# Second attention: 64-row scores of an even and an odd head issued in pairs, without zeroed queries

## The chip, the cores and the metric

One core of one Trainium2 chip. The metric is the time of the program on the device in microseconds. The kernel before ran three times: median 1390.95 us, from 1390.49 to 1391.43.

## The reference, cut to what matters

Three layers run over one sequence of 256 tokens of width 1024: an attention layer with latent projections (MLA), a MoBA attention layer, and a third layer of gated linear attention beside grouped-query attention, followed by a mixture of 64 experts. The change touches the attention of the second layer. With 256 tokens there is one key block, so that what counts of it is plain causal attention of 16 heads of 64 values:

```python
s_own = jnp.einsum('bhcd,bhkd->bhck', qq, k_own).astype(jnp.float32) * scale
s_own = jnp.where(k_pos[None, :] <= q_pos[:, None], s_own, -jnp.inf)
p = jax.nn.softmax(jnp.concatenate([s_sel, s_own], axis=-1), axis=-1).astype(qq.dtype)
...
return (o * jax.nn.silu(gate)) @ w_o
```

Each score is a sum over 64 values, half of the 128 rows of the TensorE array.

## The kernel before, in words

The program is written as one instruction stream for each engine, with semaphores between them; nothing is reordered by a planner. The order on every engine is the order of the lines that it runs.

**Work of an attention.** `attention(kind, ...)` (L1831 for TensorE, L1246 for VectorE, `softmax_units`, L841, for ScalarE) runs over units; a unit is one head and one tile of 128 queries. Kind "a" is the first attention, "b" the second (32 units: 0 to 15 are the 16 heads of tile 0 with 128 keys, 16 to 31 those of tile 1 with 256 keys), "g" the third (16 units, all with 256 keys). In loop step u TensorE issues
- the scores of unit u (L1840, one fp32 product, which the trace shows as two matmuls), and for "a" and "b" a bf16 matmul of the identity with the causal mask onto the last 128 keys (L1842, all 128 rows),
- the transposes of the probabilities of unit u-3 (L1768, after the exponentials of that unit),
- what is written beside this step: transposes of mixed outputs and pieces of the output projection (`project_piece`, L1813), in 15 steps from 18 to 35,
- the product of probabilities and values of unit u-4 (L1867, after VectorE has copied the transposed probabilities).

VectorE in step u takes the row maximum of the scores of unit u (L1252), then copies the transposed probabilities of unit u-3 to SBUF (L1076), then what is written beside (splits of weights, L1115 and L1120, and drains of transposed outputs), and after each eighth unit scales the outputs (L1267, L1270). ScalarE takes the exponentials (L853).

**Score banks.** Scores go to PSUM banks in rotation (`score_bank_of`, L452): four banks for units 0 to 15, three for units 16 to 31 of "b", since one bank is then used by the output projection. From unit 4 on the scores of a unit wait until the exponentials of the last user of its bank are done.

**Pairs.** For kind "g" alone, `paired` (L1846) makes the even step issue the scores of units u and u+1; the odd step issues none. There the scores have no mask, and an even head takes rows 0 to 63 and an odd head rows 64 to 127 of both operands.

**Queries of "b".** `heads_out` (L1221) writes the transposed keys with two heads in 128 rows, so `k_b` holds heads 2c and 2c+1 in column c. The queries are laid out with one column for each head, in `q_b` of 16 columns: `queries_out` (L1382) copies the even heads of a tile into rows 0 to 63 of the even columns and the odd ones into rows 64 to 127 of the odd columns, by two VectorE copies of 64 rows. GpSimd has zeroed the other halves before (`zero_other_heads`, L685, two memsets, L691). The scores (`scores_b`, L2012) then take all 128 rows, and the other head's keys meet zeros.

**Around it.** Before the attention TensorE runs the projections of `moba_w_in` (L1813) with the transposes of the queries between them; behind it come the rest of the output projection, the layer norm, the third layer, the router, and the experts (L2231, L2251). Weights come by DMA, issued on SyncE's queue when a projection has given its ring slot free (L539) or an expert has been used (L633, L552, L556).

Of the kernel before, what the change touches and what calls it, by code (L numbers as in the profile page):

```python
# [26 lines left out]
P = 128  # L27
D = 1024
SEQ = 256
TILES = SEQ // P  # L30
KD = D // P

H = 16
# [3 lines left out]
HD = 64  # L37
# [54 lines left out]
JOB = {job: n for n, job in enumerate(JOBS)}  # L92
# [95 lines left out]
def build(nc, t):  # L188

    where, const_cols = const_layout()  # L190
    with ExitStack() as ctx:
# [3 lines left out]
        def sem(name):  # L195
            return ctx.enter_context(nc.semaphore(name))
# [3 lines left out]
        tr_bank = bank[2:4]  # L200
# [71 lines left out]
        q_t, k_t = qk[:, 0:4096], qk[:, 4096:8192]  # L272
        q_a = q_t.rearrange("p (h s) -> p h s", h=H)
        k_a = k_t.rearrange("p (h s) -> p h s", h=H)
        q_b = q_t.rearrange("p (h s) -> p h s", h=H)
        k_b = k_t[:, 0:2048].rearrange("p (h s) -> p h s", h=H // 2)
        ln_row = tmp

# [63 lines left out]
        proj_in_psum = sem("proj_in_psum")  # L342
        proj_in_sbuf = sem("proj_in_sbuf")
        tr_in_psum = sem("tr_in_psum")
        tr_in_sbuf = sem("tr_in_sbuf")
        masks_cast = sem("masks_cast")
        q_b_zeroed = sem("q_b_zeroed")
        power_set = sem("power_set")
        rsqrt_asked = sem("rsqrt_asked")
        rsqrt_done = sem("rsqrt_done")  # L350
# [312 lines left out]
        @block.gpsimd  # L663
        def _(pool):
            def scale_gla_heads(r, n):

                pool.wait_ge(rsqrt_done, n + 1)
                for tile in range(TILES):
                    o = wide[:, tile, 0:512]
                    o3 = o.rearrange("p (h d) -> p h d", h=4)  # L670
                    nc.gpsimd.tensor_tensor(o3, o3, r[:, 4 * tile:4 * tile + 4].rearrange(
                        "p (h a) -> p h a", a=1).to_broadcast([P, 4, GDV]), ALU.mult).then_inc(gla_normed, 1)
                    pool.wait_ge(gla_normed, tile + 1)
                    nc.gpsimd.tensor_tensor(o, o, gate[:, tile, 0:512], ALU.mult).then_inc(gla_gated, 1)

            def gate_outputs(kind):

                for n in range(4):
                    tile, group = n // TILES, n % TILES
                    half = slice(512 * group, 512 * group + 512)  # L680
                    pool.wait_ge(out_drained, OUT0[kind] + n + 1)
                    nc.gpsimd.tensor_tensor(wide[:, tile, half], wide[:, tile, half], gate[:, tile, half],
                                            ALU.mult).then_inc(mixed_ready, 1)

            def zero_other_heads():  # L685

                pool.wait_ge(proj_in_psum, JOB["moba_w_in", 0, 1] + 1)
                pairs = q_b.rearrange("p (c two) s -> p c two s", two=2)
                for odd in range(2):
                    rows = slice(HD * (1 - odd), HD * (2 - odd))  # L690
                    nc.gpsimd.memset(pairs[rows, :, odd, :], 0.0).then_inc(q_b_zeroed, 1)  # L691

            nc.gpsimd.memset(power[:], -0.5).then_inc(power_set, 1)
            pool.wait_ge(power_set, 1)
            for name, (n, a, w) in RSQRT.items():
                if name in ("ln0t0", "ln1t0"):
                    gate_outputs("a" if name == "ln0t0" else "b")
                pool.wait_ge(rsqrt_asked, n + 1)
                nc.gpsimd.tensor_tensor(rstd[:, a:a + w], var[:, a:a + w], power[:, 0:w], ALU.pow).then_inc(  # L699
                    rsqrt_done, 1)  # L700
                if name == "ln0t1":
                    zero_other_heads()
                if name == "gla":
                    scale_gla_heads(rstd[:, a:a + w], n)

# [340 lines left out]
        def _(dve):  # L1046
# [20 lines left out]
            tr = [0]  # L1067
# [63 lines left out]
            for half in range(2):  # L1131
                for tile in range(TILES):
                    n = TILES * half + tile
                    dve.wait_ge(x_hi_drained, n + 1)
                    at = (slice(None), slice(4 * half, 4 * half + 4), slice(tile * P, tile * P + P))
# [18 lines left out]
            for k in range(2):  # L1154
                g = head_gain[:, HD * k:HD * k + HD]
                pairs = g.rearrange("p (d two) -> p d two", two=2)
                scale = HD ** -0.5 if k == 0 else 1.0
                for tile in range(TILES):
                    at = slice(HD * tile, HD * tile + HD)
                    cos, sin = const("cos_g")[:, at], const("sin_g")[:, at].rearrange("p (d two) -> p d two", two=2)  # L1160
                    nc.vector.scalar_tensor_tensor(rope_g[:, 2 * k, at], cos, scale, g, ALU.mult, ALU.mult)
                    for x in range(2):
                        dst = rope_g[:, 2 * k + 1, at].rearrange("p (d two) -> p d two", two=2)[:, :, x]
                        last = nc.vector.scalar_tensor_tensor(dst, sin[:, :, x], scale, pairs[:, :, 1 - x],
                                                              ALU.mult, ALU.mult)
# [67 lines left out]
            for i in range(4):  # L1233
                last = nc.vector.tensor_copy(
                    stage[:, i, :].rearrange("p (h d) -> p h d", h=4)[:, :, NOPE:QKD],
                    key_rope[:, i % 2:i % 2 + 1, :].to_broadcast([P, 4, ROPE]))
# [144 lines left out]

            def queries_out(n):  # L1382

                b, tile = n // TILES, n % TILES
                dve.wait_ge(tr_in_psum, tr[0] + 1)
                pairs = q_b[:, 8 * b:8 * b + 8, tile * P:tile * P + P].rearrange("p (c two) s -> p c two s", two=2)
                for odd in range(2):
                    rows = slice(HD * odd, HD * odd + HD)
                    last = nc.vector.tensor_copy(pairs[rows, :, odd, :],
                                                 tr_bank[tr[0] % 2][rows, :].rearrange("p (c s) -> p c s", s=P))  # L1390
                last.then_inc(tr_in_sbuf, 1)
                tr[0] += 1

            split_lo(block_of(("moba_w_in", 2, 0)))
            for n in range(4):
# [52 lines left out]
            for tile in range(TILES):  # L1448
                at = slice(HD * tile, HD * tile + HD)
# [5 lines left out]
                for kv in range(KVH):  # L1455
                    last = nc.vector.tensor_copy(
                        key2[:, tile, 128 * kv:128 * kv + 128].rearrange("p (c d) -> p c d", c=2),
                        att_kv[:, tile, HD * kv:HD * kv + HD].rearrange("p (c d) -> p c d", c=1).to_broadcast(
                            [P, 2, HD]))
# [298 lines left out]
        def _(pe):  # L1758
            tr = [0]
# [71 lines left out]
            def attention(kind, units, depth, scores, values, beside):  # L1831
                def score(u):
                    h, tile = unit_of(kind, u)
                    keys = keys_of(kind, tile)
                    dst = score_bank_of(kind, u)
                    if u >= 4:
                        pe.wait_ge(probs_done, UNIT0[kind] + score_bank_before(kind, u) + 1)
                    lhs, rhs = scores(h, tile, keys)
                    causal = kind != "g"
                    last = nc.tensor.matmul(dst[:, 0:keys], lhs, rhs, start=True, stop=not causal)  # L1840
                    if causal:
                        last = nc.tensor.matmul(dst[:, keys - P:keys], ident_b[:], causal_b[:],  # L1842
                                                start=False, stop=True)
                    last.then_inc(scores_in_psum, 1)

                paired = kind == "g"  # L1846
                for u in range(units + depth + 1):
                    if u < units and not (paired and u % 2):
                        score(u)
                        if paired:  # L1850
                            score(u + 1)
                    m = u - depth
                    if 0 <= m < units:
                        pe.wait_ge(probs_done, UNIT0[kind] + m + 1)
                        transposes([probs[:, m % 4, P * k:P * k + P]
                                    for k in range(keys_of(kind, unit_of(kind, m)[1]) // P)])
                    if u in beside:
                        beside[u]()
                    m = u - depth - 1
                    if m >= 0:  # L1860
                        h, tile = unit_of(kind, m)
                        pe.wait_ge(tr_in_sbuf, tr_of_unit(kind, m) + 1)
                        if m % 8 == 0 and m >= 16:
                            pe.wait_ge(out_drained, OUT0[kind] + m // 8 - 1)
                        blocks = keys_of(kind, tile) // P
                        for k in range(blocks):
                            last = nc.tensor.matmul(out_bank[m // 8 % 2][:, HD * (h % 8):HD * (h % 8) + HD],  # L1867
                                                    probs_t[:, m % 2, P * k:P * k + P], values(h, k),
                                                    start=(k == 0), stop=(k == blocks - 1))
                        if m % 8 == 7:  # L1870
                            last.then_inc(out_in_psum, 1)
# [138 lines left out]
            pe.wait_ge(proj_in_sbuf, JOB["moba_w_in", 3, 1] + 1)  # L2010

            def scores_b(h, tile, keys):  # L2012
                return q_b[:, h, tile * P:tile * P + P], k_b[:, h // 2, 0:keys]

            pe.wait_ge(q_b_zeroed, 2)
            attention("b", UNITS_B, 3, scores_b, values_ab, first_output("b", "moba_w_o"))
            rest_of_output("b", "moba_w_o", "w_in_2", 1)

# [369 lines left out]
```

## Time and profile before

| | before |
|---|---|
| median of 3 runs | 1390.95 us |
| the profiled execution, its time | 1389.75 us |
| its span in the trace | 1387.9 us |
| PE busy | 1043.4 us (75%) |
| VectorE busy | 478.4 us (34%) |
| ScalarE busy | 282.8 us (20%) |
| GpSimd busy | 36.1 us (3%) |
| granted TensorE clock, mean | 0.909 |
| HBM read | 462.07 MB |

All times below are us from the start of the span, durations are us unless ns is written. PE is the matmul side of TensorE, PEld its loads of stationary operands, which run beside it. In a timeline a row is start, duration, engine, line, operation, tiles, count, and in brackets the idle time of the engine before it with its releaser. A merged row of matmuls (x2, x8) lasts from the first start to the last end; the ends of matmuls are modelled and reach beyond the start of the next. In the chain of waits a row is start, length, and the piece of work that held the end at that time; there the lengths of neighbours do not overlap. In the table of windows the columns are the window, its length, busy time with count of PE, PEld, VectorE, ScalarE and GpSimd, granted clock, DMA share and GB/s.

### The profile page before, as it was taken

To read this page: it belongs to the slowest core of one execution; us is meant where nothing else is said; L and a number is where in the kernel's file an instruction comes from. 1 tells how busy PE (TensorE), PEld (TensorE's weight loads), DVE (VectorE), ACT (ScalarE), POOL (GpSimd) and SP (SyncE) were. 2 spreads that over 40 slices of the span, in tenths; PEclk is the share of its full clock that TensorE was granted. 3 is DMA by queue.
4 is the path that set the end of the run, shared out by engine and by line. 5 is a ranking of instruction groups with operands and counts; after the bars stand their busy time and mean duration, and the time that the engine had idled before them with its cause. 6 is when DMAs were issued, how large, how long until landed. Compare 5 with 4: busy or idle time off the path is not lost.

```text
span 1387.9 us, 21666 instructions
## 1 busy us (share of the span) xinstructions
PE 1043.4 (75%) x9215; PEld 656.9 (47%) x9215; DVE 478.4 (34%) x1052; ACT 282.8 (20%) x610; POOL 36.1 (3%) x34
## 2 busy tenths in 40 slices
PE   8999999999999885674756756566665756747566
PEld 6857778778766542332423423233232423324232
DVE  4456784786954431121212212021120211212122
ACT  5334343544732111010000000010010110100000
POOL 0000101011102000000000000000000000000000
PEclk9999999999999999898888888898897988978888
DMA  8462255403575699999999999999999999999995
GB/s 309 137 243 70 73 201 181 156 27 131 185 306 248 246 378 424 428 427 424 428 426 425 428 427 424 428 426 425 428 425 428 425 425 427 427 425 427 428 423 246
DMA packets 69808, 463.75 MB, mean 334 GB/s; under 512 B 6722, under 2 KB 15108, under 8 KB 36356
## 3 DMA queue, kind: packets, MB, share of 16 engines
q1 hardware_dynamic: 68976, 460.48, 81.0%
q10 hardware_dynamic: 788, 2.66, 0.6%
q8 instruction: 31, 0.51, 0.1%
q14 instruction: 13, 0.11, 0.0%
HBM read 462.07 MB, written 1.05 MB: 334 GB/s over the span
## 4 chain that ended last, share of the span: by engine, by line
DMA 47%; PE 43%; DVE 6%; ACT 1%; issue 1%; SPq 1%; POOL 0%; DVEq 0%; ACTq 0%
DMA ring<-in_w_up 46%; PE bank L2231 14%; PE bank L1813 13%; PE bank L1796 5%; PE bank L1768 3%; PE bank L1867 2%; PE bank L1840 2%; PE bank L2251 1%; PE bank L1888 1%; SPq L552 1%; DVE ring_lo L1115 1%; PE bank L2305 1%; DVE ring_lo L1120 1%; PE bank L2213 1%; DMA res<-in_x 0%
## 5 line engine op out<-in xcount | busy, mean ns | idle before, releaser
L2231 PE MATMUL bank<-ring,expert_area 128*32 128x256 f32 x3968 | 324.0, 493 | 219.1 <-DMA ring<-in_w_up 217.8
L2231 PEld LDWEIGHTS bank<-ring,expert_area 128*32 128x32 f32 x3968 | 149.5, 137 | 386.4 <-DMA ring<-in_w_up 238.5
L1813 PE MATMUL bank<-ring_lo,xt_hi 128*128 128x512 f32 (+3 forms) x576 | 182.8, 386 | 0.6 <-DVE small L1305 0.4
L1650 DVE TENSOR_TENSOR expert_area<-expert_area,bank 128x128 f32<-128x128 f32 x64 | 18.2, 285 | 469.2 <-ACT expert_area L1008 469.2
L1008 ACT ACTIVATE expert_area<-bank 128x128 f32<-128x128 f32 x64 | 17.7, 277 | 617.7 <-PE bank L2231 617.7
L2251 PE MATMUL bank<-ring,consts 128*32 128x256 f32 x2016 | 121.8, 382 | 27.9 <-DVE consts L1652 27.9
L1813 PEld LDWEIGHTS bank<-ring_lo,xt_hi 128*128 128x128 f32 x576 | 104.1, 188 | 20.6 <-issue 3.7
L2251 PEld LDWEIGHTS bank<-ring,consts 128*32 128x32 f32 x2016 | 62.2, 109 | 69.3 <-DVE consts L1652 20.1
L1813 PE MATMUL bank<-ring_lo,xt_lo 128*128 128x512 f32 (+2 forms) x240 | 91.2, 380 | 0.0
L1796 PE MATMUL bank<-ring,xt 128*128 128x384 f32 (+1 forms) x192 | 75.7, 541 | 1.4 <-DVE xt L1079 0.8
L1656 DVE COPY consts<-bank 32x256 f32<-32x256 f32 x63 | 26.5, 421 | 132.8 <-PE bank L2251 132.8
L2305 PE MATMUL bank<-consts,expert_area 128*128 128x512 f32 x120 | 55.1, 601 | 16.2 <-DVE consts L1657 16.2
L1012 ACT COPY consts<-bank 32x256 f32<-32x256 f32 x63 | 22.7, 360 | 203.9 <-PE bank L2251 203.9
L2213 PEld LDWEIGHTS bank<-consts,wide 128*128 128x128 f32 x480 | 56.0, 192 | 7.2 <-issue 7.2
L2213 PE MATMUL bank<-consts,wide 128*128 128x128 f32 x480 | 56.0, 275 | 0.0
L2243 PE MATMUL bank<-consts,expert_area 128*128 128x128 f32 x64 | 21.0, 328 | 46.1 <-DVE expert_area L1650 46.1
L1115 DVE TENSOR_TENSOR ring_lo<-ring,ring_lo 128x2048 fp32r<-128x2048 f32 (+2 forms) x23 | 47.5, 2082 | 21.4 <-ACT ring_lo L762 21.2
L1674 DVE TENSOR_TENSOR res<-res,bank 128x512 f32<-128x512 f32 x60 | 41.2, 687 | 26.9 <-PE bank L2305 26.9
L1796 PEld LDWEIGHTS bank<-ring,xt 128*128 128x128 f32 x192 | 35.0, 190 | 30.5 <-issue 16.7
L1813 PEld LDWEIGHTS bank<-ring_lo,xt_lo 128*128 128x128 f32 x240 | 45.1, 188 | 8.5
L699 POOL TENSOR_TENSOR rstd<-var,power 128x1 f32<-128x1 f32 (+3 forms) x15 | 17.4, 1160 | 1102.0 <-DVE var L1744 919.4
L2243 PEld LDWEIGHTS bank<-consts,expert_area 128*128 128x128 f32 x64 | 8.9, 139 | 74.1 <-DVE expert_area L1650 74.1
(286 smaller groups left out, 1174.3 us busy)
## 6 DMA issues: line engine op xcount, KB each, us to landing
ring<-in_w_down SPq DMA_DIRECT2D x62, 2048.0 KB, 24.7
ring<-in_w_gate SPq DMA_DIRECT2D x61, 2048.0 KB, 18.3
ring<-in_w_up SPq DMA_DIRECT2D x60, 2048.0 KB, 22.8
ring<-in_moba_w_kv SPq DMA_DIRECT2D x4, 2048.0 KB, 8.3
ring<-in_moba_w_in SPq DMA_DIRECT2D x4, 2048.0 KB, 8.7
ring<-in_w_in SPq DMA_DIRECT2D x3, 2048.0 KB, 7.8
ring<-in_mla_w_uq SPq DMA_DIRECT2D x4, 1152.0 KB, 5.7
ring<-in_mla_w_o SPq DMA_DIRECT2D x2, 2048.0 KB, 8.0
```

The lines of the kernel that those rows point to most:

```text
L1115: last = nc.vector.tensor_tensor(lo[:, at], w[:, at], hi[:, at].bitcast(F32), ALU.subtract)
L1674: nc.vector.tensor_tensor(dst, dst, bank[5 + k % 3][:], ALU.add).then_inc(sum_added, 1)
L1768: last = nc.tensor.transpose(tr_bank[n % 2][0:cols, P * i:P * i + rows], x, ident[0:rows, 0:rows])
L1796: last = nc.tensor.matmul(proj_bank[n % 2][:, 0:width], xt[:, first + c, tile * P:tile * P + P], w[:, c, :], start=(c == 0), stop=(c == kc ...
L1813: last = nc.tensor.matmul(dst, x[at], w[:, c, :], start=(piece == 0 and c == 0 and w is hi and x is xt_hi), stop=(piece == 1 and c == 3 an ...
L1840: last = nc.tensor.matmul(dst[:, 0:keys], lhs, rhs, start=True, stop=not causal)
L1867: last = nc.tensor.matmul(out_bank[m // 8 % 2][:, HD * (h % 8):HD * (h % 8) + HD], probs_t[:, m % 2, P * k:P * k + P], values(h, k), start ...
L2213: last = nc.tensor.matmul(bank[c // 4][:, P * (c % 4):P * (c % 4) + P], routed[:, tile, c, :], onehot[:, tile, :], start=(tile == 0), stop ...
L2231: last = nc.tensor.matmul(bank[2][SLOTS * j:SLOTS * j + SLOTS, 0:256], picked[:, c, SLOTS * i:SLOTS * i + SLOTS], both[:, :, c, j // 2, j ...
L2243: nc.tensor.transpose(bank[3][:, 256:384], hidden, ident).then_inc(hidden_t_in_psum, 1)
L2251: last = nc.tensor.matmul(bank[4][SLOTS * j:SLOTS * j + SLOTS, 0:256], hidden_t[:, SLOTS * k:SLOTS * k + SLOTS], w[:, k, 256 * j:256 * j + ...
L2305: nc.tensor.matmul(bank[5 + k % 3][:], back[:, P * tile:P * tile + P], expert_out[:, 512 * half:512 * half + 512], start=True, stop=True). ...
```

## The change

The second attention treats its scores as the third one does. `q_b` shrinks to 8 columns of two heads, the zeros and the semaphore for them go, the queries leave PSUM by the same helper as the keys (one copy of 128 rows for each of the four transposed groups in place of two of 64), the scores take 64 rows of both operands, and the scores of units u and u+1 are issued in one even step. The mask matmul stays with each score, so that a pair is: scores of the even head (rows 0 to 63), mask (128 rows), scores of the odd head (rows 64 to 127), mask (128 rows).

```diff
-        q_b = q_t.rearrange("p (h s) -> p h s", h=H)
+        q_b = q_t[:, 0:2048].rearrange("p (h s) -> p h s", h=H // 2)
...
-            def zero_other_heads():
-
-                pool.wait_ge(proj_in_psum, JOB["moba_w_in", 0, 1] + 1)
-                pairs = q_b.rearrange("p (c two) s -> p c two s", two=2)
-                for odd in range(2):
-                    rows = slice(HD * (1 - odd), HD * (2 - odd))
-                    nc.gpsimd.memset(pairs[rows, :, odd, :], 0.0).then_inc(q_b_zeroed, 1)
...
-                if name == "ln0t1":
-                    zero_other_heads()
...
             def queries_out(n):
 
-                b, tile = n // TILES, n % TILES
-                dve.wait_ge(tr_in_psum, tr[0] + 1)
-                pairs = q_b[:, 8 * b:8 * b + 8, tile * P:tile * P + P].rearrange("p (c two) s -> p c two s", two=2)
-                for odd in range(2):
-                    rows = slice(HD * odd, HD * odd + HD)
-                    last = nc.vector.tensor_copy(pairs[rows, :, odd, :],
-                                                 tr_bank[tr[0] % 2][rows, :].rearrange("p (c s) -> p c s", s=P))
-                last.then_inc(tr_in_sbuf, 1)
-                tr[0] += 1
+                heads_out(q_b, n, 4, P)
...
-                paired = kind == "g"
+                paired = kind != "a"
...
             def scores_b(h, tile, keys):
-                return q_b[:, h, tile * P:tile * P + P], k_b[:, h // 2, 0:keys]
-
-            pe.wait_ge(q_b_zeroed, 2)
+                at = slice(HD * (h % 2), HD * (h % 2) + HD)
+                return q_b[at, h // 2, tile * P:tile * P + P], k_b[at, h // 2, 0:keys]
+
```

## Rows read from the trace of the kernel before

**Rows 1.** The page, the chain that ended last, by engine

```profile
DMA 47%; PE 43%; DVE 6%; ACT 1%; issue 1%; SPq 1%; POOL 0%; DVEq 0%; ACTq 0%
```

**Rows 2.** Windows: before, in the second attention, in the third, among the experts

```profile
213.00:271.00 58.00, 57.80 (x258) 46.67 (x256) 35.51 (x36) 23.02 (x21) 3.61 (x2) 1.00 0.49 172
271.50:282.20 10.70, 10.10 (x85) 9.19 (x86) 7.61 (x30) 7.70 (x31) 1.27 (x1) 1.00 0.46 148
407.70:426.00 18.30, 16.95 (x124) 12.46 (x124) 13.80 (x39) 11.77 (x51) 6.79 (x6) 1.00 1.02 431
500.00:560.00 60.00, 42.81 (x506) 24.68 (x498) 16.82 (x39) 7.28 (x16) 0.00 (x0) 0.94 0.95 398
```

**Rows 3.** Chain of waits in the second attention, tile 0, then tile 1

```profile
274.41 0.28 PE bank L1840 x2
...
275.75 0.28 PE bank L1840 x2
276.03 0.06 PE bank L1842
276.09 0.12 PE bank L1768
276.20 0.17 PE bank L1867 x2
...
279.45 0.69 DVE wide L1270
...
297.92 0.49 PE bank L1840 x2
```

**Rows 4.** Timeline of the second attention: a copy and the product that waited for it

```profile
274.98 0.28 DVE L1076 COPY probs_t<-bank 128x128 f32<-128x128 f32 x1
...
275.32 0.43 PE L1867 MATMUL bank<-val,probs_t 128*128 128x64 f32 x2
```

**Rows 5.** Timeline of PE, 64-row matmuls between projections: 256 columns

```profile
383.51 0.39 PE L1813 MATMUL bank<-ring_lo,xt_lo 128*128 128x512 f32 x1
...
384.20 0.39 PE L1813 MATMUL bank<-ring_lo,xt_lo 128*128 128x512 f32 x1
384.52 1.14 PE L2074 MATMUL bank<-val,qk 64*128 64x256 f32 x8
...
386.15 0.40 PE L1813 MATMUL bank<-ring_lo,xt_lo 128*128 128x512 f32 x1
```

**Rows 6.** The same with 128 columns

```profile
394.96 0.40 PE L1813 MATMUL bank<-ring_lo,xt_lo 128*128 128x512 f32 x1
395.29 0.72 PE L2089 MATMUL bank<-qk 64*128 64x128 f32 x8
...
396.51 0.39 PE L1813 MATMUL bank<-ring_lo,xt_lo 128*128 128x512 f32 x1
```

**Rows 7.** Timeline of the third attention: a pair of scores, and the load behind

```profile
415.12 0.70 PE L1840 MATMUL bank<-qk 64*128 64x256 f32 x4
...
415.75 0.20 PEld L1768 LDWEIGHTS bank<-consts,probs 128*128 128x128 f32 x2 [0.33 <-issue]
```

**Rows 8.** Groups by form, 271 to 316: loads of the scores and of the mask

```profile
L1840 PEld LDWEIGHTS bank<-qk 128*128 128x128 f32 x64 | 9.8, 193 | 1.2 <-issue 1.1
...
L1842 PEld LDWEIGHTS bank<-causal_b,ident_b 128*128 128x128 bf16 x32 | 3.2, 99 | 0.4
```

**Rows 9.** Waits, 271.4 to 314.4: PE for copies of transposed probabilities

```profile
PE bank L1768 <- DVE probs_t L1076: 1.6, 3, 0.8
```

**Rows 10.** Timeline: the zeros on GpSimd, the first two groups of query copies

```profile
235.66 3.67 POOL L691 MEMSET qk<- 64x2048 f32 x2 [56.34 <-PE bank L1813]
...
241.71 2.81 DVE L1389 COPY qk<-bank 64x512 f32<-64x512 f32 x4 [3.29 <-PE bank L1768]
```

**Rows 11.** Behind it: an expert load issued, and the chain's first wait for one

```profile
473.96 0.33 SPq L633 DMA_DIRECT2D ring<-in_w_gate  x1
...
520.48 20.65 DMA ring<-in_w_up
```

More of the change, by code:

```diff
@@ L346, in build @@
         masks_cast = sem("masks_cast")
-        q_b_zeroed = sem("q_b_zeroed")
         power_set = sem("power_set")
```

## The prediction

> **What bounds the kernel now.** I read the page's chain first. Waiting for weights holds 47% of it and PE 43% [rows 1], so a change to PE's order can reach the end only where PE and not the weights hold the chain. The chain in order of time has its first wait for an expert's weights at 520.48 [rows 11]; from 271 to there it runs through PE, VectorE and short hand-offs. The loads that later pace the experts are issued when TensorE has used a buffer, the first such at 473.96 [rows 11]. What the second attention gains or loses therefore moves the experts' loads and the end by as much. Second, the windows. Up to 271 PE is busy 57.80 of 58.00 us, and in the second attention (271.5 to about 315) it is busy 10.10 of 10.70 us, at a granted clock of 1.00, that is 2.4 GHz [rows 2]. Third, the chain inside it. A unit of tile 0 is 0.28 for the scores, 0.06 for the mask, 0.12 for a transpose and 0.17 for the values, and two units take 1.34 (274.41 to 275.75); the values of every second unit come late, since they wait for the copy that ends at 275.26 and start at 275.32 [rows 3, 4]. So PE bounds tile 0, with VectorE's copy close behind. In tile 1 the scores cost 0.49, PE still leads, and where VectorE has splits of weights beside, PE waits 1.6 us in all for copies [rows 3, 9].
>
> **The removed work.** The zeros are 3.67 us of GpSimd at 235.66, and each query copy is 0.70 us: two groups are 2.81 [rows 10]. Halving the copies frees 4 x 0.70 = 2.8 us of VectorE. Both lie in the window where PE is 99% busy [rows 2], so I cost them at nothing. If that cover were gone, at most 2.8 us would come back. The semaphore for the zeros was met 30 us before it was asked. No DMA is moved; the loads wait on later PE work and shift with it.
>
> **Does the pair overlap?** In the third attention four matmuls of 256 columns and 64 rows last 0.70 [rows 7], against 2 x 0.49 for two such units in series [rows 3]. The two halves do run side by side there. Here a mask of 128 rows stands between the heads and takes both halves, and matmuls start in order, so I expect no overlap and no stream gets shorter. The Trainium skill (TensorEngine Tiling, Theoretical Speedup) gives up to 2x for a contraction of 64 or less; the rival below says what that would make of the time. It is told for tiles that run beside each other, and the mask denies that here.
>
> **What the halves cost.** A 64-row block between 128-row matmuls is not free. From one L1813 matmul to the third behind it takes 0.69 (383.51 to 384.20), with the block between 1.95 (384.20 to 386.15) [rows 5]. The block costs 1.26, and its work is four streams of 256 columns (eight matmuls, two at a time), 4 x 0.245 = 0.98 by the step of rows 3. That leaves 0.28 for going in and coming out. With 128 columns it is 1.55 - 0.69 = 0.86 against 4 x 0.14 = 0.56, leaving 0.30 [rows 3, 6]. The load behind a pair shows why: it stands 0.33 idle until the 64-row matmuls are nearly through, where 128-row loads go ahead under the running matmul [rows 7]. The same page of the Trainium skill (Key Properties) says that a change of tiling mode drains TensorE, and by that rule, the trace agrees.
>
> The change puts a 64-row stretch of two matmuls before every mask, so each of 32 units goes in and out once. Before it there were none. The cost e of one unit is 0.30 by rows 5 and 6. Low end: the mask's load is bf16 and lasts 99 ns where a score's lasts 193 [rows 8], and coming out exposes that load: 0.28 - 0.10 = 0.18. High end: inside a block a stream may need no more than 512 cycles of 2.4 GHz, 0.213 (L1813 does 512 columns in 0.69 / 3 = 0.23 [rows 5]), which leaves 1.26 - 0.85 = 0.41, say 0.43 with rows 6 (0.86 - 4 x 0.107). I take 0.30, for it comes out of both blocks by steps that were measured.
>
> **The order costs too.** With both scores in the even step, the transpose of unit u-3 comes after them, and the values of u-3 follow in the next step with only a transpose and one product between. In tile 0 the pair becomes: 2 x (0.28 + 0.06 + e) = 1.28, transpose to 1.40, hand-off 0.05, copy 0.28, hand-off 0.06, and values from a standstill 0.43 [rows 3, 4], together 2.22 against 1.34. That is 0.88 more, of which 0.28 would be there with e at zero. The values of u-4 and the transpose of u-2 hide under the copy.
>
> **Sum.** Tile 0: six full periods (pairs at steps 4 to 14), 6 x 0.88 = 5.3. The first four units have no copy to wait for, 4 x 0.30 = 1.2. The scaling of outputs, 0.69 on the chain at 279.45 [rows 3], falls into the longer period: minus 0.7. Together 5.8. Tile 1: 16 x 0.30 = 4.8, and here PE has pieces and longer transposes between, so that the order itself costs nothing; the 1.6 us that PE now waits for copies [rows 9] take up part, leaving 3.2. In all 9.0, or 32e - 0.6. The profiled execution would go from 1389.75 to 1398.8. The median of the three runs lies 1.2 above that execution, so the median goes from 1390.95 to **1400.0**. With e at 0.18 the sum is 5.2, with 0.43 it is 13.2: 1396.1 to 1404.2.
>
> **A new wait.** From unit 18 on three banks rotate. In step u the scores of u+1 now need the exponentials of u-2, and they stand ahead of the transpose of u-3, all values behind it and so VectorE's copies. I cost it at nothing: between the scores of u-2 and those of u+1 PE has two transposes and two products of values, over 1.2 us, beside the drains and pieces. If a split on VectorE comes between, what is late is the maximum of u-2.
>
> **The rivals.**
> 1. *The masks do not stop the overlap, and no border costs* (not slower). Place: the pair of scores. For it speaks the 0.70 of rows 7. Tile 0 gains nothing: 0.28 + 0.12 + 0.12 + 0.05 + 0.28 + 0.06 + 0.43 = 1.34, the copy sets the old period. In tile 1 each pair saves 0.49, 3.9 in all, less the 1.6 of rows 9, where VectorE leads already: 1388.6. It decides only if e is under about 0.1. Against it: the 0.33 of rows 7 at a border of just this kind.
> 2. *Only the order costs.* Borders free, no overlap: 6 x 0.28 = 1.7, 1392.7. Against it: rows 5 and 6.
> 3. *The bank wait holds.* Seven even steps from 18, each 0.5 to 1.0 where a split delays the maximum: 3.5 to 7 on top, 1403.5 to 1407. For it: the 1.6 us of rows 9 show VectorE late in some steps; against it, the distance above.
> 4. *The clock falls.* At 500 to 560, where PE stands waiting for weights, the mean grant is 0.94 [rows 2]; a stretch at 1.2 GHz through these 50 us would add some 20 us: 1420. Against it: the third attention, with two borders to a pair and waits, is granted 1.00 [rows 2].
>
> **How the numbers follow.** A measurement here can tell about 0.2%, 2.8 us. My forecast gets 0.79, rival 1 0.05, rival 2 0.06, rival 3 0.07, rival 4 0.03. The range reaches over the bounds of e and a little of rivals 2 and 3: 1395.5 to 1404.5. Slower by over 0.2% is the forecast with rivals 3 and 4, 0.89. Within 0.2% are rivals 1 and 2, less what of rival 1 could reach over 2.8 us: 0.09. Faster: 0.02.
>
> **What the new profile would show.** In the second attention the loads of the masks and of the scores stand idle 0.1 to 0.35 us before them, as in rows 7. The period of a pair in tile 0 is about 2.2 us. The stretch from the first score to the last scaling of outputs is 9 us longer than now. The window before it is as long as now, and everything behind is the same, shifted by 9. Scores of an even and an odd head that start together would prove rival 1; a period of 1.6 rival 2; PE standing before a score and released by ScalarE rival 3; a grant under 1.00 between 271 and 325 rival 4. The sum is wrong if the shift from 325 to 520 shrinks, that is if something there was waiting for a transfer.

## The result, and the profile after

The changed kernel takes 1409.62 us (median of four executions, 1407.37 to 1413.85) against 1391.19 before: 1.0136 times, 95% interval 1.0112 to 1.0161. It is 18.4 us slower. I had forecast 1400.0 with a range to 1404.5, so the direction was right and the size was wrong. Ratios here and below leave out executions more than 1.5% above the fastest of their kernel, which the medians do count: three of the kernel with 64 rows alone (1424.0 to 1426.5 us) and one of the kernel with the transpose first (4406 us at a mean grant of 0.204, cause unknown).

| | before | after |
|---|---|---|
| median | 1391.19 us | 1409.62 us |
| the profiled execution: time, span | 1389.75, 1387.9 us | 1409.76, 1407.9 us |
| PE busy | 1043.4 us | 1065.8 us |
| VectorE busy | 478.4 us | 476.4 us |
| GpSimd busy | 36.1 us | 32.4 us |
| granted clock, mean | 0.909 | 0.896 |
| first load that an expert sets free | 473.96 | 494.35 |

The lines of the new file are some 20 lower: the scores are L1821, the mask L1823, transposes L1749, values L1848, projection pieces L1794, and the copy of transposed probabilities L1065.

The windows first, one of the kernel before and then the kernel after:

```profile
275.00:279.00 4.00, 4.00 (x38) 3.82 (x37) 2.88 (x13) 2.75 (x12) 0.00 (x0) 1.00 0.45 164
```

```profile
213.00:271.00 58.00, 58.00 (x263) 47.16 (x260) 32.89 (x33) 23.49 (x20) 0.00 (x0) 1.00 0.49 174
271.50:275.00 3.50, 2.83 (x14) 1.85 (x14) 1.00 (x4) 3.12 (x8) 0.00 (x0) 0.85 0.66 193
275.00:279.00 4.00, 4.00 (x16) 2.95 (x15) 1.46 (x6) 1.38 (x6) 0.00 (x0) 0.50 0.61 226
306.00:310.00 4.00, 4.00 (x19) 3.27 (x18) 3.41 (x5) 0.57 (x2) 0.27 (x1) 0.74 0.00 0
310.00:314.00 4.00, 4.00 (x26) 3.02 (x25) 2.50 (x7) 2.19 (x6) 0.00 (x0) 1.00 0.00 0
428.00:446.00 18.00, 16.65 (x122) 12.18 (x122) 13.61 (x39) 11.79 (x51) 6.78 (x6) 1.00 1.02 431
```

The granted clock, the third number from the end, is what I had not expected. The grant is 1.00 up to the attention and 0.50, that is 1.2 GHz, from 274 on, until it comes back near 307, when pieces of the projection stand between the units. In the kernel before it is 1.00 from 271.5 to 350. The third attention (428 to 446) is granted 1.00, as before. PE counts as busy 4.00 of 4.00 us at half the clock: busy time does not show the loss, the count does: 16 matmuls in these 4 us, 38 in the kernel before. Part of that difference is the borders and the order, the rest the clock.

The chain of waits of the kernel after, in order of time (start, length, work): first units, one pair of tile 0, one score of tile 1, and a unit after the clock is back.

```profile
272.79 0.42 PE bank L1821 x2
273.20 0.16 PE bank L1823
...
278.24 0.72 PE bank L1821 x2
278.96 0.22 PE bank L1823
279.18 0.72 PE bank L1821 x2
279.91 0.22 PE bank L1823
280.13 0.22 PE bank L1749
280.34 0.32 PE bank L1848 x2
280.67 0.21 PE bank L1749
280.88 0.54 PE bank L1848 x2
281.42 0.72 PE bank L1821 x2
...
294.14 1.15 PE bank L1821 x2
...
309.53 0.63 PE bank L1821 x2
310.16 0.16 PE bank L1823
```

At full clock a score and its mask now hold the chain for 0.42 + 0.16 in tile 0 and 0.63 + 0.16 in tile 1, where they held it for 0.28 + 0.06 and 0.49 + 0.06 [rows 3]. That is 0.24 more for each unit, my e. At half clock the same pieces are 0.72 + 0.22 and 1.15 + 0.22, and a pair of tile 0 takes 3.18 (278.24 to 281.42) against 1.34.

The timeline of PEld, after, shows the border that I had read from the third attention [rows 7]:

```profile
278.89 0.10 PEld L1823 LDWEIGHTS bank<-causal_b,ident_b 128*128 128x128 bf16 x1 [0.22 <-issue]
```

The mask's load stands idle for 0.22 and starts when the 64-row matmuls (278.24 to 278.96 in the chain) are nearly through. The chain's first wait for an expert's weights and the first freed load moved with the stage:

```profile
540.79 20.87 DMA ring<-in_w_up
```

520.48 became 540.79 and 473.96 became 494.35 [rows 11]: 20.3 and 20.4 us, and the span grew by 20.0. So what is behind the attention took up almost none of it. Up to 271 TensorE is as busy as before. The first score starts at 272.17 against 271.53, but that is no effect of the change: the profile of the kernel with 64 rows alone, with the same code up to there, has it at 271.48.

### The profile page after: what moved, and what is told of

It is laid out like the page before. It is cut to its first block, busy times and chain, and to the rows that moved or that the text cites. A ratio compares the mean times of both kernels' runs of the same rounds, so it can differ in the third digit from the quotient of the medians.

```text
span 1407.9 us, 21660 instructions
## 1 busy us (share of the span) xinstructions
PE 1065.8 (76%) x9215; PEld 668.3 (47%) x9215; DVE 476.4 (34%) x1048; ACT 283.4 (20%) x610; POOL 32.4 (2%) x32
## 4 chain that ended last, share of the span: by engine, by line
DMA 46%; PE 45%; DVE 5%; ACT 1%; issue 1%; SPq 1%; POOL 0%; DVEq 0%; ACTq 0%
DMA ring<-in_w_up 46%; PE bank L2212 14%; PE bank L1794 13%; PE bank L1777 5%; PE bank L1749 3%; PE bank L1821 3%; PE bank L1848 2%; PE bank L2232 1%; PE bank L1869 1%; SPq L551 1%; DVE ring_lo L1104 1%; PE bank L1823 1%; PE bank L2286 1%; PE bank L2194 1%; DVE qk L1065 0%
## 5 line engine op out<-in xcount | busy, mean ns | idle before, releaser
L1794 PE MATMUL bank<-ring_lo,xt_hi 128*128 128x512 f32 (+3 forms) x576 | 183.0, 386 | 0.6 <-DVE small L1294 0.4
L1794 PEld LDWEIGHTS bank<-ring_lo,xt_hi 128*128 128x128 f32 x576 | 104.2, 189 | 20.5 <-issue 3.7
L1794 PE MATMUL bank<-ring_lo,xt_lo 128*128 128x512 f32 (+2 forms) x240 | 91.2, 380 | 0.0
L1821 PE MATMUL bank<-qk 64*128 64x256 f32 (+3 forms) x160 | 48.8, 427 | 1.6 <-DVE qk L1065 0.8
L1794 PEld LDWEIGHTS bank<-ring_lo,xt_lo 128*128 128x128 f32 x240 | 45.1, 188 | 8.5
L842 ACT ACTIVATE probs<-bank,small 128x256 f32<-128x256 f32 (+1 forms) x80 | 34.4, 431 | 60.0 <-DVE small L1241 53.9
```

The lines of the kernel that those rows point to most:

```text
L842: nc.scalar.activation(probs[:, u % 4, 0:keys], score_bank_of(kind, u)[:, 0:keys], ACT.Exp, bias=neg_max[:, n:n + 1], accum_out=row_sum[:, ...
L1794: last = nc.tensor.matmul(dst, x[at], w[:, c, :], start=(piece == 0 and c == 0 and w is hi and x is xt_hi), stop=(piece == 1 and c == 3 an ...
```

## The experiments

Thirteen kernels, in the order in which they ran. Ratios are against the kernel before on the same chip. For each kernel one trace was kept, that of the profiled execution; of the others the time and the mean grant over the whole program are known. The expectations name four theories of why the clock falls: A, the array does too little in a given time; B, the order of the pairs; C, the ways in and out of 64 rows; D, half of the rows lying idle.

| | median us | spread | ratio, 95% interval |
|---|---|---|---|
| order alone | 1391.74 | 1390.6 to 1393.0 | 1.0014 [1.0005, 1.0024] |
| 64 rows alone | 1407.77 | 1393.6 to 1426.5 | 1.0083 [1.0048, 1.0118] |
| masks behind both scores | 1393.33 | 1390.3 to 1394.1 | 1.0016 [1.0006, 1.0026] |
| 64 rows for 8 units | 1391.33 | 1388.9 to 1391.6 | 1.0006 [0.9996, 1.0015] |
| the changed kernel again | 1408.67 | 1408.1 to 1409.2 | 1.0134 [1.0117, 1.0151] |
| filled with transposes | 1398.44 | 1397.7 to 1411.0 | 1.0078 [1.0048, 1.0108] |
| 128 rows, made to stand | 1395.07 | 1394.4 to 1396.0 | 1.0037 [1.0022, 1.0051] |
| masks behind, transpose first | 1390.37 | 1388.5 to 1391.9, and 4406 | 1.0002 [0.9993, 1.0012] |
| pairs on 128 rows, made to stand | 1397.56 | 1397.2 to 1399.0 | 1.0053 [1.0037, 1.0070] |
| 64 rows in tile 0 only | 1402.78 | 1402.3 to 1404.6 | 1.0095 [1.0078, 1.0112] |
| 64 rows in tile 1 only | 1397.56 | 1393.5 to 1398.0 | 1.0043 [1.0028, 1.0057] |
| old layout, zeros and copies kept | 1411.79 | 1408.0 to 1415.7 | 1.0147 [1.0118, 1.0177] |
| other half of the rows filled | 1399.07 | 1396.5 to 1403.1 | 1.0064 [1.0040, 1.0088] |

Where a spread is wide the mean grants differ as well, from 0.883 to 0.909 with 64 rows alone: the clock falls in some executions of a kernel and not in others, or for different lengths of time.

**Order alone.** On the kernel before:

```diff
-                paired = kind == "g"
+                paired = kind != "a"
```

> The kernel before with the pairing alone: zeroed queries and 128 rows stay, the scores of two units are issued in the even step. Theory A (the 64-row scores make the array less busy, and the clock falls for that): the clock stays at 1.00 through the second attention and the time is 1.7 us longer than before, from 0 to 2.5 (the copy that a value product waits for, 0.28 a pair in tile 0). Theory B (the order, with TensorE standing for copies in every odd step, lets the clock fall): the clock falls to 0.5 in tile 0 and the time is 10 us or more longer.

It takes 1391.74 us against 1390.12, 1.6 more, at a grant of 1.00. The chain of waits of this kernel, one pair of tile 0:

```profile
275.13 0.28 PE bank L1840 x2
275.41 0.06 PE bank L1842
275.46 0.28 PE bank L1840 x2
275.74 0.06 PE bank L1842
275.80 0.13 PE bank L1768
...
275.95 0.30 DVE probs_t L1076
...
276.30 0.43 PE bank L1867 x2
276.73 0.28 PE bank L1840 x2
```

The pair takes 1.60, with transpose, copy and values one behind the other, as the working had it (1.34 + 0.28). Theory B falls: the order does not let the clock fall by itself, in none of ten executions (1390.6 to 1393.0).

**64 rows alone.** On the changed kernel:

```diff
-                paired = kind != "a"
+                paired = kind == "g"
```

> The changed kernel without the pairing: 64-row scores, one unit in each step, in and out of 64 rows with each unit. Theory A: the clock falls in tile 0, as in the changed kernel; borders (32 x 0.24 less what waits hide) and about 30 us at half the clock, 13 to 18 us longer than before. Theory B: the clock stays at 1.00, and only the borders are left, 5 to 7 us longer than before.

Both theories got part. Four of ten executions took 1393.6 to 1395.5, 4.7 us over before by their middle, and the profiled one (1394.68) is among them; its grant is 1.00 throughout. The other six took 1407.8 to 1426.5 at mean grants of 0.883 to 0.900; no trace of them was kept, so that where and for how long their clock was at half is not shown. The chain of the profiled one, one unit of tile 0:

```profile
275.70 0.41 PE bank L1821 x2
276.12 0.16 PE bank L1823
276.28 0.12 PE bank L1749
276.39 0.17 PE bank L1848 x2
276.56 0.41 PE bank L1821 x2
```

A unit is 0.86. The same pieces were 0.63 before [rows 3], so e is 0.23 without any pairing. Whether the clock falls differs here from one execution to the next; with pairs and 64 rows together all eight executions (four here, four below) took 1407 us or more. In the profiled one the clock had fallen by the fourth score (273.94, 0.68 long), before the pairs change the order of anything on TensorE, so that there the pairs did not start the fall. Whether they make it likelier, these counts suggest and do not prove.

**Masks behind both scores.** On the changed kernel:

```diff
                         score(u)
                         if paired:
                             score(u + 1)
+                        if kind == "b":
+                            mask(u)
+                            mask(u + 1)
```

(`score` leaves the mask matmul to `mask` for this kind.)

> The changed kernel with both masks behind both scores of a pair: score even, score odd, mask even, mask odd. If the mask between the heads keeps them apart, the two scores now start within 0.05 us of each other, there is one way in and one out for a pair, and a pair of tile 0 needs no more than now. With the clock at 1.00 the time is within 1 to 3 us above before. If the clock falls in spite of it (theory A: still fewer columns of the array at work in the same time), 8 to 14 us above before.

The timeline of PE of this kernel:

```profile
275.05 0.49 PE L1821 MATMUL bank<-qk 64*128 64x128 f32 x4
275.48 0.28 PE L1831 MATMUL bank<-causal_b,ident_b 128*128 128x128 bf16 x2
```

Four matmuls of two heads last 0.49, where two of one head lasted 0.46 to 0.49 in the changed kernel: the halves run side by side once no mask stands between. The three lowest executions are at 1390.3 to 1391.6, about level with before; the median is 3.2 over, just outside what I had expected. The profiled one, 1393.7, lost the clock for some 7 us near the end of the stage (310 to about 317), after PE had stood for VectorE:

```profile
306.00:310.00 4.00, 2.27 (x16) 1.57 (x15) 4.00 (x10) 1.54 (x6) 0.00 (x0) 0.94 0.00 0
310.00:314.00 4.00, 3.97 (x14) 3.52 (x15) 1.93 (x4) 0.15 (x2) 0.00 (x0) 0.50 0.76 259
```

So moving the masks takes 15 of the 18 us back, but no more: it is not faster than the kernel before.

**64 rows for eight units.** On the kernel before, with its zeros and its layout:

```diff
             def scores_b(h, tile, keys):
-                return q_b[:, h, tile * P:tile * P + P], k_b[:, h // 2, 0:keys]
+                at = slice(HD * (h % 2), HD * (h % 2) + HD) if h % 4 == 0 else slice(0, P)
+                return q_b[at, h, tile * P:tile * P + P], k_b[at, h // 2, 0:keys]
```

> The kernel before with 64 rows for the scores of every fourth head only (8 of 32 units; zeros, order and copies as before). Theory A: eight units at 0.24 us for the two borders, less a little that waits hide: 1.2 to 2.0 us longer, the clock stays at 1.00. If a single stretch of 64 rows is enough to let the clock fall: 8 us or more.

1.2 us by the medians, though the interval reaches to no change, and the grant stays at 1.00. Eight borders with work of 128 rows between did not bring the clock down.

**The changed kernel again.**

> The changed kernel itself, unaltered, in more executions. If rows and order together always let the clock fall, all ten take 1407 us or more. If it is a matter of chance as with 64 rows alone (four of ten executions at 1393.6 to 1395.5), some take 1396 to 1399, which would be the price with the clock at full: 7.1 by 32e - 0.6 with e at 0.24.

Four executions, 1408.1 to 1409.2. None stands near the 1396 to 1399 of a kept clock, and the mean grants are 0.897 and 0.898. In the profiled one the clock fell later than in the first profile, about 5 us after the first score (272.13 to 277.10).

**Filled with transposes.** On the changed kernel, the transposes of odd steps under 20 are made four times, with the same result:

```diff
+                for i, x in list(enumerate(blocks)) * times:
...
+                                   4 if kind == "b" and u % 2 and u < 20 else 1)
```

> The changed kernel with the transpose in odd steps below 20 made four times in place of once (the same result each time), in the place where TensorE otherwise stands for a copy. Theory A (the clock falls because the array does too little in tile 0): the clock stays at 1.00 or falls later and for less time, and though more work is done the time falls, to 1397 to 1402. Theory C (the clock falls for the ways in and out of 64 rows, whatever else is done): no less than the changed kernel, 1408 to 1412.

Four of six executions took 1397.7 to 1398.8 and two 1410.2 and 1411.0. The four, at mean grants of 0.905 to 0.908, are some 10 us faster than the changed kernel though they do more work, as theory A had it; the two are where theory C had them, and the only trace, of the 1411.0, shows the clock at half from about 275 on. More work on 128 rows makes the fall less frequent and does not rule it out. The gap of 12.6 us between the groups is one price of the fall, by times alone.

**128 rows, made to stand.** On the kernel before:

```diff
                     last.then_inc(scores_in_psum, 1)
+                    if kind == "b":
+                        pe.wait_ge(scores_in_psum, UNIT0[kind] + u + 1)
```

> The kernel before (zeroed queries, 128 rows, one unit in a step), with TensorE made to wait after each score and mask until both are finished, some 0.2 to 0.3 us each. Theory A: such standing counts as much as that at a border, so the clock falls in some executions, as with 64 rows alone, and the time is spread over 1394 to 1425. Theory D (half of the rows at work is what counts): the clock stays at 1.00, all executions within 2 us of each other, 4 to 8 us above before.

1394.4 to 1396.0, all within 1.6 us, grant 1.00. The chain of waits of this kernel, a unit of tile 0:

```profile
276.83 0.28 PE bank L1840 x2
277.11 0.07 PE bank L1842
277.18 0.04 issue
...
277.72 0.28 PE bank L1840 x2
```

A unit is 0.89, a little longer than the 0.86 of 64 rows alone, which lost the clock six times in ten. Standing as long on full rows did not lose it in five. This speaks for theory D and against standing as the cause.

**Masks behind, transpose first.** On the kernel with the masks behind, the transpose of unit u-3 goes ahead of the scores on TensorE, and its copy ahead of the maximum on VectorE in even steps:

```diff
                 for u in range(units + depth + 1):
+                    if kind == "b":
+                        turn(u - depth)
                     if u < units and not (paired and u % 2):
...
+                    if kind == "b" and u % 2 == 0:
+                        copy(u - depth)
```

> Masks behind both scores of a pair, and in even steps the transpose of unit u-3 ahead of the scores, with VectorE's copy of it ahead of the maximum, so that the copy runs under the scores. With the clock at 1.00: a pair of tile 0 needs 0.42 + 0.18 + 2 x 0.12 + 2 x 0.17 = 1.18 against 1.34, one of tile 1 0.63 + 0.18 + 2 x 0.23 + 2 x 0.39 = 2.05 against 2.34, 1 to 3.5 us under before. If the clock falls, some us above.

No difference from before that can be told: 1.0002. A pair of tile 0 takes 1.26 against 1.34 (275.37 to 276.63 in its chain), where 1.18 was expected, but where VectorE holds the chain (its splits, and the scaling of outputs) shorter pairs of TensorE bring nothing. I had expected 1 to 3.5 us under the kernel before; it equals it.

**Pairs on 128 rows, made to stand.** The wait of the kernel "128 rows, made to stand", together with the order of the change.

> The kernel before with the order of the change (two units in the even step) and TensorE made to wait after each score and mask until they are finished, all on 128 rows with zeroed queries. A pair of tile 0 then takes about as long as one of the changed kernel at full clock, 2.0 to 2.2 us, with about as little streaming. Theory D (the half of the rows at work is what lets the clock fall): the clock stays at 1.00, all executions within 2 us of each other, 6 to 9 us above before. Theory A (streaming in too little of the time, whatever the rows): the clock falls in tile 0, 1405 us or more in most executions.

1397.2 to 1399.0, grant 1.00. A pair of tile 0 takes 2.14 here (277.02 to 279.16 in the chain), about what the changed kernel would need at full clock. With the same order and nearly the same length of a pair, on 128 rows, the clock holds in all four executions. Half of these rows meet zeros, so it is not useful products that count, but rows taken.

**64 rows in one tile only.** As with eight units, the condition being `tile == 0` or `tile == 1`, with pairs for all units.

> Zeroed queries in their old layout, the order of the change for all units, and 64 rows for the scores of tile 0 alone. If the clock falls only through tile 0 and comes back when the scores take 128 rows again or the first projection piece is reached, it is at half for 20 us or so, and the time is 10 to 15 us above before; with the clock at full it would be 5 us above.

> As the last, with 64 rows for the scores of tile 1 alone. There a pair has twice the columns, longer transposes and pieces of the projection in most steps. Borders of 16 units, 16 x 0.24 less the 1.6 that waits hide, and the order in tile 0, 1.2 to 1.7: 3 to 4 us above before, the clock at 1.00. If rows alone let the clock fall, 8 us or more.

Tile 0 only: 12.5 us over before, within the 10 to 15 expected, the grant at half through tile 0 and back when the scores take 128 rows again (windows of that kernel):

```profile
271.50:275.00 3.50, 3.50 (x22) 2.45 (x21) 1.74 (x7) 3.02 (x11) 0.00 (x0) 1.00 0.93 303
279.00:291.00 12.00, 12.00 (x47) 8.89 (x46) 4.49 (x16) 3.29 (x15) 1.27 (x1) 0.50 0.00 0
298.00:302.00 4.00, 4.00 (x27) 3.30 (x26) 3.97 (x8) 1.13 (x4) 1.28 (x1) 1.00 0.00 0
```

Tile 1 only: 7.3 us by the medians, in five executions from 1393.5 (3.2 over, what I expected at full clock) to 1398.0. I had expected the clock to stay; in the profiled execution it fell within 3 us of the first 64-row score (282.77 to about 285.7 in its chain) and came back with the pieces of the projection, while in the kernel of tile 0 it had come back before any piece of the projection:

```profile
283.00:287.00 4.00, 3.90 (x17) 2.03 (x15) 1.67 (x5) 1.32 (x5) 0.00 (x0) 0.82 0.02 4
287.00:291.00 4.00, 4.00 (x17) 2.84 (x15) 2.45 (x6) 0.80 (x4) 0.00 (x0) 0.50 0.00 0
295.00:299.00 4.00, 4.00 (x21) 2.94 (x20) 2.38 (x5) 1.07 (x4) 0.00 (x0) 0.90 0.00 0
```

**Old layout, zeros and copies kept.** The kernel before with pairs and 64-row scores out of the zeroed layout.

> 64-row scores in pairs as in the changed kernel, but with the queries in their old layout, the zeros on GpSimd and two copies for each group left in. If the removed zeros and copies are worth nothing, as forecast, it stands at the changed kernel's 1407 to 1410 us; if they were worth their 2.8 us of VectorE, 1410 to 1413.

1408.0 to 1415.7, with 1408.0 twice and 1415.6 and 1415.7. The two low ones stand at the changed kernel's time; in the profiled one (1415.71) the clock stayed at half until 320, longer than in the changed kernel (307). The four executions leave a gain of 2.8 us open; against it speaks that PE is busy 57.27 of 58.00 us from 213 to 271 here, so that the window before the attention is nearly as full with the zeros and copies as without.

**Other half of the rows filled.** On the changed kernel, each score of units 0 to 13 gets a second one on the other 64 rows, whose result is overwritten; a wait keeps it off a bank that is still read:

```diff
+                    if kind == "b" and u < 14 and u + 1 >= 4:
+                        pe.wait_ge(probs_done, UNIT0[kind] + score_bank_before(kind, u + 1) + 1)
                     last = nc.tensor.matmul(dst[:, 0:keys], lhs, rhs, start=True, stop=not causal)
+                    if kind == "b" and u < 14:
+                        at = slice(HD * (1 - h % 2), HD * (2 - h % 2))
+                        nc.tensor.matmul(score_bank_of(kind, u + 1)[:, 0:keys], q_b[at, h // 2, tile * P:tile * P + P],
+                                         k_b[at, h // 2, 0:keys], start=True, stop=True)
```

> The changed kernel, with each score of units 0 to 13 accompanied by a score of the other half of the rows, written to the bank of the next unit, where it is overwritten later. Both halves then work at the same time; the ways in and out of 64 rows stay, four for a pair, and so does the time of a pair. Theory D (half of the rows at work lets the clock fall): the clock stays at 1.00 in tile 0 and falls, if at all, in tile 1 only, for 10 us or so: 1397 to 1403. Theory C (the ways in and out let it fall): it falls in tile 0 as in the changed kernel, 1407 to 1414.

The timeline of PE and then the windows of this kernel:

```profile
275.92 0.37 PE L1823 MATMUL bank<-qk 64*128 64x128 f32 x1
275.93 0.37 PE L1826 MATMUL bank<-qk 64*128 64x128 f32 x1
276.13 0.27 PE L1823 MATMUL bank<-qk 64*128 64x128 f32 x1
276.14 0.27 PE L1826 MATMUL bank<-qk 64*128 64x128 f32 x1
```

```profile
279.00:283.00 4.00, 3.80 (x32) 2.79 (x32) 2.49 (x10) 1.64 (x7) 0.41 (x1) 1.00 0.00 0
283.00:287.00 4.00, 3.80 (x22) 2.49 (x21) 1.94 (x8) 1.58 (x8) 0.86 (x1) 1.00 0.00 0
287.00:291.00 4.00, 3.90 (x17) 2.00 (x16) 1.39 (x5) 1.70 (x6) 0.00 (x0) 0.70 0.00 0
291.00:295.00 4.00, 4.00 (x16) 3.00 (x14) 3.17 (x8) 0.56 (x2) 0.00 (x0) 0.50 0.00 0
```

The second score starts 0.01 us behind the first, and does not lengthen the pair. The ways in and out are all there (a pair takes 2.10 us, from 275.41 to 277.51 in its chain), yet the grant is 1.00 as long as both halves work. It falls some 6 us after the last filled unit (282.7 to 288.6 in the chain), in the unfilled ones. With the borders and the order unchanged, filling the idle half keeps the clock; with full rows and as much standing (the two kernels made to stand) it holds as well. So of the differences between the kernels it is the idle half of the rows that brings the clock down. Not settled is how it works together with the rest: fewer borders (eight units) or other work between them (the repeated transposes) keep the clock in all or some executions, and whether idle rows would bring it down without the gaps at the borders was not tried. Theory A in the form "too little streaming, whatever the rows" is out by the kernels made to stand; in the form "too little of the array at work" these kernels do not tell it from theory D. Its two lowest executions, 1396.5 and 1397.9, are 6.5 and 7.9 over before, and by their mean grants, 0.908 and 0.911, they lost little or no clock; no trace of them was kept.

## Why the prediction was wrong

**Where the shift goes: right.** The stage's loss came out at the end almost whole, 20.4 us at the first freed load and 20.0 in the span of the profiled executions.

**What bounds tile 1: misread.** "In tile 1 the scores cost 0.49, PE still leads" holds for part of it. The chain of waits of the kernel before runs through VectorE from 284.6 to 293.0 and from 299.7 to 309.0, but for hand-offs, mostly in the splits of weights:

```profile
288.79 1.78 DVE ring_lo L1115
...
303.04 1.69 DVE ring_lo L1120 x2
```

There a longer unit of TensorE is at first hidden: with 64 rows alone, at full clock, VectorE holds 10.9 us of the chain between 281 and 325 where it held 19.1. The first four units were counted at a full border each as well, but before the change the chain goes there through ScalarE (271.45 to 273.21). Both make the sum too high, by little.

**The removed work: as forecast, as far as shown.** VectorE has four copies of 0.69 fewer and is 2.0 us less busy in all, GpSimd 3.7, and TensorE is as busy up to 271. The kernel with the old layout does not prove that they were worth nothing.

**No overlap across the mask: right.** In the changed kernel a second head's matmuls start after the first mask; with the masks behind they start together.

**What the halves cost: mechanism right, size off.** I took e as 0.30 within 0.18 to 0.43; it is 0.24, of which 0.13 to 0.14 lies in the score and 0.10 in the mask. The 0.30 came from longer blocks with an fp32 load behind them; that the mask's shorter bf16 load makes the difference is likely and was not tried by itself. By my own sum, 32e - 0.6, this makes 7.1 us, and the executions that seem to have kept the clock lie near it: 6.5 and 7.9 with the other half filled, and 6.3 by the first two kernels, 4.7 for the rows plus 1.6 for the order.

**The order: right.** A pair of tile 0 takes 1.60 with the order alone (working: 1.62), and 2.10 with the borders in the kernel with the other half filled (2.10 by the working with e at 0.24). The new bank wait is not there: in the list of waits of the kernel after, the scores' loads waited 0.2 us in all for the exponentials, and their matmuls not at all. Rival 3 is out.

**The failed step: rival 4.** The sum has no term for the clock, and I gave its fall 0.03, "against it: the third attention, with two borders to a pair and waits, is granted 1.00". The comparison did not hold. There the two heads of a pair run side by side and fill both halves of the rows; here the mask keeps them apart, a fact that I had written down under "Does the pair overlap?" and did not carry over to the clock. What is left of the 18.4 us, 18.4 - 7.1 = 11.3 (12.1 with the 6.3 of the first two kernels), is put down to the clock. The rows are of that size: six periods of 3.18 in place of 2.10 are 6.5, and six units of tile 1 at 1.15 + 0.22 in place of 0.63 + 0.16 are 3.5, together 10.0, not counting the other steps at half clock, and counting tile 1 as if VectorE had nowhere been in the way. The two groups of the kernel filled with transposes give 12.6.

My price for that rival, 20 us, was for 50 us at half; it was 33.

The trace shows PE busy 4.00 of 4.00 us at a grant of 0.50: the busy share of a profile does not tell whether the clock will hold. The Trainium skill (TensorE: Matmul & The Clock Gate, The HAM clock gate) says that activity releases the throttle, and by that page one would look for an idle TensorE. For this fall the measurement decides, and it shows none but the 0.78 us ahead of the first score, which the kernel before has too (0.73) at a grant of 1.00.

## What to carry to other kernels

Before giving matmuls half of the rows, ask what stands between the two halves: here a matmul of 128 rows between them took the overlap away and cost 0.24 us for going in and out of each unit, and with half of the rows idle the clock was at half for 33 us. Put the full-row matmuls of a group behind all half-row ones, which cost 3.2 us here in place of 18.4, or keep zeros and full rows: no kernel here was clearly faster than that. When a stage becomes less dense, read the grant of the stage in the profile after, and compare it only with stages that fill the array in the same way.

## What was not expected

The clock went to half while PE counted as fully busy, within 2 us of the first 64-row score in one profile of the changed kernel (272.17 to 273.94) and 5 us in the other, and came back without any pause when 128-row scores or projection pieces returned. With 64 rows alone it fell in six of ten executions, with pairs besides in all eight, by their times, and on 128 rows with about equal standing in none of nine. A second matmul on the idle half starts 0.01 us after the first and does not lengthen the pair; filling work of this kind, or repeated transposes, made a kernel that does more finish about 10 us sooner. What the grant depends on beyond this, and why it fell for some 7 us in the profiled execution of the kernel with the masks behind, stays open.
